# Gate rows and sums of squares on TensorE: from 4-row and 4-column matmuls to the whole array

## The reference, cut to what matters

```python
def mlstm_chunkwise(q, k, v, li, lf):       # 4 heads of width 256
    # F = cumsum(lf), G = running max of (li - F), one value for each head and token
    # weight of token s for token t is exp(-(G[t] - (li - F)[s])), causal
    ...
    den = jnp.sum(s_qk, axis=-1) + ...      # one value for each head and token
    hj = num / jnp.maximum(jnp.abs(den), jnp.exp(-m_row))[..., None]
...
hm = hm * jax.nn.sigmoid(heads(p['ml_o'], ML_HEADS))
y_ml = rmsnorm(hm, ml_norm_g.reshape(ML_HEADS, ML_HD))      # mean of squares over 256 features of a head
la = jax.nn.log_sigmoid(p['gla_a'] @ gla_w_a + gla_b_a) / GLA_TAU   # rank 16
```

## Time and profile before

| | |
|---|---|
| median of 3 runs | 2288.04 us |
| the profiled execution's own time | 2286.69 us |
| its span, first to last instruction | 2284.9 us |
| TensorE busy | 2210.3 us (97%) |
| VectorE, ScalarE, GpSimd busy | 50%, 42%, 41% |
| granted TensorE clock, mean | 0.995 of full |

### The profile page before, as it was taken

How to read it: one execution, slowest core, us unless ns; L and a number is a source line. 1 busy time by engine, 2 the same in 40 slices (tenths; PEclk the granted TensorE clock), 3 DMA queues, 4 the chain that set the end, 5 groups by cost and what they waited for, 6 DMA issues and landing times. The chain is left out here.

```text
span 2284.9 us, 35526 instructions
## 1 busy us (share of the span) xinstructions
PE 2210.3 (97%) x14670; PEld 1709.9 (75%) x14670; DVE 1137.2 (50%) x1920; ACT 967.8 (42%) x1392; POOL 928.0 (41%) x711
## 2 busy tenths in 40 slices
PE   7999999999999999999999998989999999999997
PEld 5776677777877867777878777776766788888885
DVE  5554843334345538333342767764544657216425
ACT  5433355445244323554452356634366243222243
POOL 3342243334543413433344446623323455545543
PEclk9999999999999999999999999999999999999999
DMA  4221222112222202222223310002121233233322
GB/s 153 90 91 39 65 89 77 65 65 83 96 87 74 98 28 79 87 66 74 65 84 116 100 32 4 5 32 94 65 65 60 79 102 102 92 96 98 102 93 74
DMA packets 50556, 175.00 MB, mean 77 GB/s; under 512 B 6036, under 2 KB 7004, under 8 KB 50396
## 3 DMA queue, kind: packets, MB, share of 16 engines
q1 hardware_dynamic: 50396, 172.73, 23.4%
HBM read 170.60 MB, written 2.11 MB: 76 GB/s over the span
## 5 line engine op out<-in xcount | busy, mean ns | idle before, releaser
L349 POOL TENSOR_TENSOR w_low<-work,w_high 128x512 fp32r<-128x512 f32 x622 | 834.8, 1364 | 1244.1 <-ACT w_high L298 1244.1
L279 PE MATMUL ps<-x_high_tiles,w_high 128*128 128x512 f32 x1544 | 624.2, 404 | 17.9 <-POOL w_low L349 10.2
L298 ACT ACTIVATE w_high<-work 128x1024 fp32r<-128x1024 f32 x311 | 329.2, 1058 | 732.7 <-PE ps L279 729.0
L279 PE MATMUL ps<-x_low_tiles,w_high 128*128 128x512 f32 x1544 | 603.5, 391 | 0.8 <-DVE x_low_tiles L371 0.8
L279 PE MATMUL ps<-x_high_tiles,w_low 128*128 128x512 f32 x1544 | 602.8, 390 | 0.0
L279 PE MATMUL ps<-arena_parts,w_high 128*128 128x512 f32 x1264 | 398.7, 392 | 4.3 <-DVE arena L437 1.6
L279 PEld LDWEIGHTS ps<-x_high_tiles,w_high 128*128 128x128 f32 x1544 | 290.7, 188 | 119.4 <-issue 44.6
L279 PEld LDWEIGHTS ps<-x_low_tiles,w_high 128*128 128x128 f32 x1544 | 290.5, 188 | 64.0 <-DVE x_low_tiles L371 1.6
L279 PEld LDWEIGHTS ps<-x_high_tiles,w_low 128*128 128x128 f32 x1544 | 290.8, 188 | 63.1 <-issue 6.0
L279 PEld LDWEIGHTS ps<-arena_parts,w_high 128*128 128x128 f32 x1264 | 238.1, 188 | 57.2 <-issue 3.2
L279 PE MATMUL ps<-arena_parts,w_low 128*128 128x512 f32 x608 | 237.3, 390 | 0.0
(11 more groups left out here) (452 smaller groups left out, 2784.2 us busy)
## 6 DMA issues: line engine op xcount, KB each, us to landing
work<-w_first SPq DMA_DIRECT2D x178, 512.0 KB, 3.6
work<-w_second SPq DMA_DIRECT2D x134, 512.0 KB, 3.6
xT_sb<-xT SPq DMA_DIRECT2D x8, 256.0 KB, 6.1
outT<-arena SPq DMA_DIRECT2D x8, 256.0 KB, 2.1
arena<-distance_bias SPq DMA_DIRECT2D x4, 256.0 KB
small<-small SPq DMA_DIRECT2D x1, 815.5 KB, 4.9
arena<-consts SPq DMA_DIRECT2D x1, 544.0 KB, 3.7
base<-consts SPq DMA_DIRECT2D x1, 512.0 KB
```

The costliest lines, as they stand in the source:

```text
L279: ins = pe.matmul(out, lhsT, rhs, start=(n == 0 and k == 0 and q == 0), stop=(n == unit["granules"] - 1 and k == len(ops[i]) - 1 and q == 2))
L298: act.activation(m.wh[:, split_of(g), :], m.raw[:, raw_of(g), :], ACT.Copy).then_inc(sem["high_ready"], 1)
L349: pool.tensor_tensor(m.wl[:, split_of(g), part], m.raw[:, raw_of(g), part], m.wh[:, split_of(g), part].bitcast(F32), ALU.subtract).then_in ...
```

## The change

It replaces, in both layers, the small matmuls by ones over all 128 rows and columns of the array.

1. **Gate rows.** A new tile `spread` holds `spread_rows` (128x512, fp32r, zero but for 8 partitions) and `spread_pick` (the pick matrix in fp32r, whose rows 32 to 35 repeat rows 0 to 3). A row set is written in two parts: its fp32r rounding by ScalarE into partitions 0 to 3, and the rest (value minus rounding) by VectorE into partitions 32 to 35. One fp32r matmul then spreads a head's row. This is done for G (in `mlstm_gates`) and for the reciprocal roots (in `mlstm_norm`).
2. **Sums.** `one_column` becomes 128 partitions by 131 columns, and all sums of lines 1015, 1039 and 1124 use 128 columns of it and write all 128 partitions of the bank.
3. **Squares.** VectorE adds the two tiles of squares of a head, so that TensorE needs one matmul a head in place of two.
4. **Gate product.** `w_a` is used with all 128 rows (zero outside 36 to 51), against all 128 partitions of the tile in which `gate_rows` lies.

```diff
 # distance_bias_side, scalar (first layer's first stage)
         act.wait_ge(sem["late"], 16 * loads)
+        act.activation(m.spread_pick, m.pick, ACT.Copy).then_inc(sem["picked"], 1)
 # mlstm_gates, vector, then scalar
+        dve.wait_ge(sem["gates_act"], 2)
+        own.op(dve.tensor_tensor(m.spread_rows[32:32 + ML_H, :], G, m.spread_rows[0:ML_H, :].bitcast(F32), ALU.subtract))
         dve.wait_ge(sem["u_turned"], 1)
...
         act.wait_ge(sem["u_ready"], 1)
+        own.op(act.activation(m.spread_rows[0:ML_H, :], G, ACT.Copy))
         own.op(act.activation(em, em, ACT.Exp, scale=-1.0))
 # mlstm_side, tensor
-            pe.matmul(m.ps[:, rbank[h % 2], :], m.pick[0:ML_H, h * P:(h + 1) * P], G, start=True, stop=True).then_inc(sem["ml_rows_ready"], 1)
+            pe.matmul(m.ps[:, rbank[h % 2], :], m.spread_pick[:, h * P:(h + 1) * P], m.spread_rows, start=True, stop=True).then_inc(sem["ml_rows_ready"], 1)
...
-            pe.matmul(m.ps[0:ML_H, 5, P:S], m.one_column[:, 3 - h:7 - h], m.rs[:, h % 2, 0:S - P], start=False,
+            pe.matmul(m.ps[:, 5, P:S], m.one_column[:, 3 - h:P + 3 - h], m.rs[:, h % 2, 0:S - P], start=False,
...
-                pe.matmul(m.ps[0:ML_H, 5, 0:P], m.one_column[:, 3 - h:7 - h], w[:, 0:P], start=(h == 0), stop=False)
+                pe.matmul(m.ps[:, 5, 0:P], m.one_column[:, 3 - h:P + 3 - h], w[:, 0:P], start=(h == 0), stop=False)
 # mlstm_norm, tensor
         for h in range(ML_H):
-            for e in range(2):
-                pe.wait_ge(sem["ml_sq"], 2 * h + e + 1)
-                ins = pe.matmul(m.ps[0:ML_H, bank, :], m.one_column[:, 3 - h:7 - h], m.ml_squares[:, e, :],
-                                start=(h + e == 0), stop=(h + e == ML_H))
-            ins.then_inc(sem["ml_sum"], 1)
+            pe.wait_ge(sem["ml_pair"], h + 1)
+            pe.matmul(m.ps[:, bank, :], m.one_column[:, 3 - h:P + 3 - h], m.ml_squares[:, 0, :],
+                      start=(h == 0), stop=(h == ML_H - 1)).then_inc(sem["ml_sum"], 1)
             yield from turns(4)
         for h in range(ML_H):
-            pe.wait_ge(sem["ml_rstd"], 1)
+            pe.wait_ge(sem["ml_low"], 1)
...
-            pe.matmul(m.ps[:, bank, :], m.pick[0:ML_H, h * P:(h + 1) * P], rstd, start=True, stop=True).then_inc(sem["ml_spread"], 1)
+            pe.matmul(m.ps[:, bank, :], m.spread_pick[:, h * P:(h + 1) * P], m.spread_rows, start=True, stop=True).then_inc(sem["ml_spread"], 1)
 # mlstm_norm, scalar
+        act.activation(m.spread_rows[0:ML_H, :], rstd, ACT.Exp, scale=-0.5).then_inc(sem["ml_rstd"], 1)
         act.activation(rstd, rstd, ACT.Exp, scale=-0.5).then_inc(sem["ml_rstd"], 1)
 # mlstm_norm, vector
-        yield from turns(start + 2 * ML_H)
+        yield from turns(start)
+        for h in range(ML_H):
+            dve.wait_ge(sem["ml_sq"], 2 * h + 2)
+            dve.tensor_tensor(m.ml_squares[:, 0, :], m.ml_squares[:, 0, :], m.ml_squares[:, 1, :], ALU.add).then_inc(sem["ml_pair"], 1)
+            yield from turns(2)
...
         yield from turns(2)
+        dve.wait_ge(sem["ml_rstd"], 2)
+        dve.tensor_tensor(m.spread_rows[32:32 + ML_H, :], rstd, m.spread_rows[0:ML_H, :].bitcast(F32), ALU.subtract).then_inc(sem["ml_low"], 1)
         for h in range(ML_H):
             dve.wait_ge(sem["ml_spread"], h + 1)
 # gla_side, tensor
-            ins = pe.matmul(AB[i], m.c1("w_a", 256)[32:64, i * P:(i + 1) * P], m.gate_rows, start=True, stop=True)
+            ins = pe.matmul(AB[i], m.c1("w_a", 256)[:, i * P:(i + 1) * P], m.pick, start=True, stop=True)
 # constants set by GpSimd at the start
-        scalars += [(m.one_column[:, n:n + 1], float(n == 3)) for n in range(7)]
+        scalars += [(m.one_column[:, 0:3], 0.0), (m.one_column[:, 3:4], 1.0), (m.one_column[:, 4:P + 3], 0.0), (m.spread_rows.bitcast(F32), 0.0)]
```

More of the change, by code:

```diff
@@ L888, in distance_bias_side @@
         bounce.append((9, ("late", 16 * (loads + 1)), m.bias_toep[:, h, :], src))
-    return Side(["vec_ready", "vec_copied", "flip_ready", "flipped"], tensor, scalar, lambda dve, sem: iter(())), bounce
+    return Side(["vec_ready", "vec_copied", "flip_ready", "flipped", "picked"], tensor, scalar, lambda dve, sem: iter(())), bounce
 def mlstm_rows(m):
@@ L1010, in head_rows @@
                 pe.wait_ge(sem["ml_arg_ready"], T * (h - 1))
-            pe.matmul(m.ps[:, rbank[h % 2], :], m.pick[0:ML_H, h * P:(h + 1) * P], G, start=True, stop=True).then_inc(sem["ml_rows_ready"], 1)
+            pe.matmul(m.ps[:, rbank[h % 2], :], m.spread_pick[:, h * P:(h + 1) * P], m.spread_rows, start=True, stop=True).then_inc(sem["ml_rows_ready"], 1)
         def sums(h):
             pe.wait_ge(sem["ml_sum_ready"], h + 1)
-            pe.matmul(m.ps[0:ML_H, 5, P:S], m.one_column[:, 3 - h:7 - h], m.rs[:, h % 2, 0:S - P], start=False,
+            pe.matmul(m.ps[:, 5, P:S], m.one_column[:, 3 - h:P + 3 - h], m.rs[:, h % 2, 0:S - P], start=False,
                       stop=(h == ML_H - 1)).then_inc(sem["ml_sum_used"], 1)
         pe.wait_ge(sem["u_ready"], 1)
-        pe.wait_ge(sem["gates_dve"], 7)
+        pe.wait_ge(sem["gates_dve"], 8)
         pe.wait_ge(sem["relu_ready"], (T - 1) * IDX_H)
+        if flips:
+            pe.wait_ge(sem["picked"], 1)
         head_rows(0)
-        pe.wait_ge(sem["gates_act"], 18)
+        pe.wait_ge(sem["gates_act"], 19)
         scores(0)
@@ L1073, in arguments @@
                               ALU.subtract, ALU.max).then_inc(sem["ml_arg_ready"], 1)
-        dve.wait_ge(sem["gates_dve"], 7)
-        dve.wait_ge(sem["gates_act"], 18)
+        dve.wait_ge(sem["gates_dve"], 8)
+        dve.wait_ge(sem["gates_act"], 19)
         if flips:
@@ L1163, in vector @@
         dve.wait_ge(sem["ml_spread_read"], ML_H)
-    return Side(["ml_sq", "ml_sum", "ml_total", "ml_log", "ml_rstd", "ml_spread", "ml_spread_read"], tensor, scalar, vector)
+    return Side(["ml_sq", "ml_pair", "ml_sum", "ml_total", "ml_low", "ml_log", "ml_rstd", "ml_spread", "ml_spread_read"], tensor, scalar, vector)
 def gla_side(m, banks, qkv_jobs, act_jobs):
@@ L2725, in build @@
         m.rs = rs
+        spread = ctx.enter_context(nc.sbuf_tensor("spread", [P, 2, S], F32R))
+        m.spread_rows, m.spread_pick = spread[:, 0, :], spread[:, 1, :]
         m.cols = sb("cols", [P, 32])
@@ L2729, in build @@
         scal = sb("scal", [P, 4])
+        m.one_column = sb("one_column", [P, P + 3])
         m.eps, m.gn_eps, m.sub_eps, m.ten_ln2 = (scal[:, n:n + 1] for n in range(4))
@@ L2737, in build @@
         m.all_ones = rs[:, 0, :]
-        m.one_column = m.cols[:, 24:31]
         m.normed = arena[:, 8:16, :]
@@ L3169, in constants @@
     put("eye64", np.tile((np.arange(P)[:, None] % 64) == np.arange(64)[None, :], (1, 1)))
-    put("pick", np.repeat(np.eye(4), P, axis=1))
+    put("pick", np.repeat(np.tile(np.eye(4), (9, 1)) * ((np.arange(36) % 32) < 4)[:, None], P, axis=1))
     rel = np.arange(640) - 511
```

## The result

The changed kernel takes 2273.15 us (median of 4 runs, 2272.16 to 2275.54), the kernel before 2287.39 (4 runs): a ratio of 0.9938, 95% interval 0.9926 to 0.995. That is 14.2 us less where 23.5 were forecast. The time is 8.7 us above the forecast and 2.1 above the range; the direction is as forecast. The profiled execution of the changed kernel took 2273.34 us, against 2286.69, so 13.35 less; what follows accounts for these.

A forecast was written before the change was run, and what follows sets the result against it. TensorE, busy 97% of the span, was taken to bound the kernel, paying for passes and array-shape changes. Gains 29.4 - 1.4 - 4.55 = 23.5 us; 2263.2 against the profiled 2286.7, plus 1.35 for the median: 2264.5 us, range 2258 to 2271.

The forecast's parts named there:

- The matmul terms: TensorE gains from fewer passes and fewer changes of array shape in both layers, 29.4 us in sum.
- the stall: TensorE waiting for VectorE's subtraction at the norm's first spread, once a layer, 4.55 us together.
- my terms for squares, roots and gate product: Second-stage gains: squares 1.14 x 8 = 9.1 us, 1.02 for each root spread, gate product 0.8 us.
- 10.0: Gains in the mLSTM part: 8 x 1.02 + 1.5 + 1.7 - 1.4 = 10.0 us.
- The spread: Spreading a gate row on TensorE: 1.25 us removed, one fp32r matmul of 0.23 added, gain 1.02 each.
- the sums of line 1045: Sums of weights (line 1039 before): 0.31 us falls to 0.22, next matmul saves 0.10; 1.5 us over 8 heads.
- The first head: Start of each mLSTM part: TensorE waits for VectorE's mask, winning 0.33 us and not 1.02; loss 1.4 us.
- A new wait: the first spread of the norm: TensorE waits once a layer for VectorE's subtraction behind the attention's work: 2.40 and 2.15 us, 4.55 together.
- My bound: Upper bound on the norm's wait: some 7 us if VectorE's 4.3 us chain is a quarter longer, 1.1 a layer.
- The stall lowers the clock: Rival: the norm's waits drop TensorE's clock, 1.7 us lost each; 2266.2 us for one, 2267.9 for two; chance 0.18.
- the row: Trace reading: TensorE once idled 2.3 us, then ran at clock 0.50 for 3.4 us; shorter idles left it full.
- a single microsecond or two for everything the shift may do to later stages: Allowance within the range 2258 to 2271 us for effects on stages behind the change.

The follow-up runs named there:

- b_squares: The kernel before with only the squares changed: VectorE adds a head's two squares, one 128-column fp32 matmul sums them; 2281.18 us, against 2289.24 on the same chip.
- a_rows36: a_early with the 16 gate-row matmuls (G and reciprocal roots) taking only rows 0 to 35, still one fp32r pass; 2270.23 us.
- b_again: The kernel before, unchanged, run once more for a second profile; 2286.61 us.
- a_again: The changed kernel, unaltered, run once more for a second profile; 2270.53 us.
- a_early: The changed kernel with the norm's subtraction moved two VectorE turns forward, ahead of the attention's work; 2264.51 us, ratio 0.9905 to before.
- a_best: a_early with 32 unread fp32 matmuls of 2 columns (weight loads of 4) added ahead of the first product; 2258.47 us, ratio 0.9869 to before.
- b_more16: The kernel before with 16 unread matmuls of 2 columns (weight loads of 4) added ahead of the first product; 2285.50 us.
- b_more48: The kernel before with 48 unread matmuls of 2 columns (weight loads of 4) added ahead of the first product; 2291.01 us.

## Why the prediction was right in direction and wrong in size

*The matmul terms were right.* Without the stall the second stages are 9.03 and 9.06 us shorter than before; my terms for squares, roots and gate product give 18.06 for both. b_squares confirmed the squares alone, a_rows36 the price of the shape. In the mLSTM part 9.5 us were gained of 10.0. The spread is not what is missing: behind fp32 matmuls the profile shows 0.31, but the last fp32 record ahead of it then shows 0.03 in place of 0.11 (205.80, 205.83, 206.15 at the second head), so that both together take 0.34 = 0.11 + 0.23. What is missing is in the sums of line 1045. I had its two records at 0.22; they stand behind a wait at every head and take 0.29 (0.32 at a layer's first), hardly less than the 0.31 before, which is 0.6 us over eight heads. The first head won 0.43 a layer where I had 0.33, which gives 0.2 back. TensorE never waits for the sum of the squares' pair: nothing in its waits names the addition.

*Failed step one: "A new wait: the first spread of the norm", sized at 2.40 + 2.15 = 4.55 us.* Place, releaser and count were right; the waits cost 5.8 us. The missing 1.2 is the chain on VectorE ahead of the subtraction: 4.95 us where the earlier trace rows gave 4.3, and 4.67 in layer two where it was 4.08. Line 1538 makes 1.0 of it, with 1.49 and 1.20 us where it took 0.97 and 0.69; the subtraction's later start behind the operation ahead of it makes the other 0.2. Line 1538 has two inputs in SBUF, and in both kernels and both layers it ends 0.55 to 0.56 us after GpSimd's first instruction of line 349 that runs beside it (427.79 to 429.06 before, 420.26 to 421.53 after): as if the rest of it began only then. The faster TensorE brought VectorE's chain forward against GpSimd's split, and so made it longer. No experiment moved line 349 alone. My bound was wide enough (a quarter longer, 1.1 us a layer); I took the durations of the kernel before as fixed.

*The rival "The stall lowers the clock"* came true in the profiled execution, for both waits, at the price named, 1.6 and 1.7 us. I gave it 0.18 and put it at nothing in the sum, because the waits would be "just under" the 2.3 us of the row and "shorter idles left the clock full". The waits were 2.8 and 2.5, over it, and the second half was misread: in the same trace of the kernel before TensorE idled 1.94 us up to 1354.56, and from 1354.8 the clock was granted at 0.50 for 3.4 us; in the changed kernel the same followed an idle time of 1.96 us at 1510.4. Nor is the drop certain at any of these lengths: b_again had the idle times of 1.94 and 2.33 us and a_again those of 2.79 and 2.49, all with a full clock behind them. So the row gave no limit to stay under, only a chance. With both losses at both places the stall took 9.1 us in that execution.

*Failed step two: "a single microsecond or two for everything the shift may do to later stages".* I treated the stages behind the change as untouched. The RWKV stage costs 3.8 us more, 2 to 5 in other executions, in the main because fewer TensorE instructions ahead of it move the places at which TensorE waits for its next block. That the places move with the instructions ahead, and the length with them, was shown by moving them without the change. The forecast's part on the change had no term for it, though "issue" stood among the waits of the kernel before in that stage.

The sum in profiled times: 23.5 forecast, less 1.2 for longer waits, 3.3 for the clock, 0.4 in the mLSTM part, 3.8 in the RWKV stage and 1.4 at the start, is 13.4; 13.35 was measured. The waits and the clock are undone by a_early, the RWKV stage's part by a_best.

*What stays open.* The place explains most of the stage's length, not all: at place 0 the executions with added matmuls took 185.2 to 185.9 where those of the kernel before as it is took 182.7 to 184.2, and at -64 they spread from 186.0 to 190.4. One part of it is the clock. In six of the twenty profiled executions (before, b_squares, b_more16, b_more48, a_again, a_best) it was granted at 0.50 for 3.4 us beginning 0.0 to 1.2 us after the start of the stage's first matmul, ahead of which TensorE is idle 1.9 us, and the stage's first 120 matmuls took 6.2 to 6.6 us; in the others they took 4.9 to 5.0. So the kernel before as profiled lost 1.7 us at this stage's start that the changed one did not; the changed one had such a stretch at 1511.3 us, near the stage's end, whose cost isn't separated. The 3.8 us of the table is therefore not the price of the places alone. At -64 this accounts for part of 188.5 (b_more48) and 189.0 (a_again); it doesn't explain the 190.4 of a_rows36, nor the 185.2 to 185.9 at place 0, whose clock was full at the stage's start. What differs in those wasn't found. Why an idle time of 1.9 to 2.8 us lowers the clock in one execution and not in the next also stays open.

## What to carry to other kernels

Where one engine is busy nearly all the time, look in its waits for idle time that has no releaser, and count the instructions between two of them: if they stand at equal distances or multiples of one, any change in the number of instructions ahead moves them, for better or worse, and a few matmuls at the start, with results that nobody reads, are a nearly free way to try other places where the engine waits for inputs anyway. A small operation that a busy engine will wait for belongs ahead of the long work in its own engine's order, in a gap where its inputs are already there; one `yield` moved was worth 5.8 us here by the wait alone, and the median fell by 8.6, nearly as much as the whole edit of the squares brought. A chain on a second engine is no fixed length either: moved against a third engine's work, it took 0.6 us longer. And price a changed array shape, not only the passes.

## What the runs showed of the hardware

- TensorE stood still for 0.3 to 2.0 us at places 254 or 256 recorded instructions apart, or near a multiple, in a stage dense with matmuls of 64 rows and columns; not at every boundary, and 9.3 to 17.1 us in all by where they fell. Each of these idle times ended 1.2 to 1.6 us after a 16 KB packet of the instruction queue had landed (before and after, 29 idle times).
- An fp32r matmul of 512 columns took 0.23 us behind its own kind. Behind an fp32 one its start is recorded early (0.03 us behind a record that takes 0.11), and both together took 0.34.
- A VectorE operation of 128x512 with two inputs in SBUF took 0.69 us alone, and 0.69 to 1.49 beside GpSimd's line 349, ending 0.55 us after GpSimd's instruction did.
- Behind idle times of 1.9 to 2.8 us the granted clock fell to 0.50 for 3.4 us in some executions and stayed full in others of the same kernel; two such drops cost 1.6 and 1.7 us.
- An fp32r matmul over 36 of 128 rows costs 0.29 to 0.39 us more than over all of them, with the same columns and passes.
- Matmuls of 2 columns with weight loads of 128 columns took 0.22 us a record (13.81 us for 64), with loads of 4 columns 0.03 (2.54 us for 96), at the start, where nothing else ran: there the time went with the load's columns.
